# Attention probabilities turned by VectorE in 32x32 squares, with products over 32 keys in eight tiles of TensorE, in a hybrid pooling, convolution and attention block

## The reference

```python
scores = einsum('bnqkgd,bnskd->bnkgqs', qb, kb)   # blocks of 128 queries, 256 keys
in_band = (dist >= 0) & (dist < 128)              # dist = query - key
scores = where(in_band & key_exists, scores - slope * dist, -1e30)
p = softmax(concatenate([scores, sink], -1))[..., :-1]
out = einsum('bnkgqs,bnskd->bnqkgd', p, vb)       # 8 query heads, 2 kv heads of 64
y_attn = out * silu(g_attn)
```

## Time and profile before

| | us |
|---|---|
| median of 3 runs | 1399.54 (1399.27 to 1400.41) |
| profiled execution, its own time | 1400.31 |
| its span | 1398.6 |
| PE busy in the span | 1376.3 (98%) |
| DVE busy | 1189.1 (85%) |
| ACT busy | 553.6 (40%) |
| POOL busy | 389.1 (28%) |

### The profile page before, as it was taken

One profiled execution on the slowest core, in us unless ns is written; L12 is line 12 of the kernel. 1 busy time (PEld: TensorE's weight loads), 2 busy tenths in 40 slices (PEclk: granted clock), 3 DMA queues, 4 the chain that ended last, 5 costly groups with the idle time before them and its releaser, 6 DMA issues.

```text
span 1398.6 us, 21036 instructions
## 1 busy us (share of the span) xinstructions
PE 1376.3 (98%) x7326; PEld 1131.5 (81%) x7326; DVE 1189.1 (85%) x2480; ACT 553.6 (40%) x1435; POOL 389.1 (28%) x592
## 2 busy tenths in 40 slices
PE   6999999999999999999999999999999999999997
PEld 4888888888888888878888888888888888888886
DVE  5887878796978786769899998988999998898886
ACT  5756565655565654512212122111231333333332
POOL 5133324233242423120101101010010455445551
PEclk9999999999999999999999999999999999999999
DMA  9716070616252426363303213032326484555431
GB/s 216 206 45 257 19 273 19 235 75 207 95 199 103 151 106 210 123 118 153 136 16 136 101 66 135 15 135 101 125 113 260 201 264 161 177 180 171 159 108 74
DMA packets 89385, 197.23 MB, mean 141 GB/s; under 512 B 13904, under 2 KB 55248, under 8 KB 81616
## 3 DMA queue, kind: packets, MB, share of 16 engines
q1 hardware_dynamic: 65152, 172.28, 34.9%
q10 hardware_dynamic: 24144, 23.80, 6.5%
HBM read 114.27 MB, written 81.79 MB: 140 GB/s over the span
## 4 chain that ended last, share of the span: by engine, by line
PE 90%; DVE 7%; DMA 1%; ACT 1%; issue 1%; POOL 0%; SPq 0%; POOLq 0%; DVEq 0%; ACTq 0%
PE wide L346 13%; PE wide L347 13%; PE wide L348 13%; PE pair L1186 6%; PE pair L1187 6%; PE pair L1192 6%; PE wide L1186 4%; PE wide L1187 4%; PE wide L1192 4%; DVE m_tail L1967 3%; PE wide L1224 2%; PE pair L1157 2%; PE turn L1144 2%; PE turn L346 2%; PE pair L346 2%; PE pair L348 2%
## 5 line engine op out<-in xcount | busy, mean ns | idle before, releaser
L1967 DVE SCALAR_TENSOR_TENSOR m_tail<-m_tail,m_taps 128x512 f32<-128x512 f32 x480 | 338.4, 750 | 4.6
L108 POOL TENSOR_TENSOR pool_carrier<-pool_carrier 128x1 f32<-128x1 f32 x77 | 29.5, 383 | 692.0 <-DVE m_meanvar L1976 398.4
L1186 PE MATMUL pair<-xT,w_hi 128*128 128x512 f32 x384 | 154.0, 401 | 4.8 <-DVE w_lo L410 4.6
L1187 PE MATMUL pair<-xT,w_lo 128*128 128x512 f32 x384 | 150.6, 392 | 0.0
L1710 POOL TENSOR_TENSOR operand_sums<-m_y 128x512 f32<-128x512 f32 x75 | 102.0, 1360 | 167.8 <-PE wide L348 116.7
L1192 PE MATMUL pair<-xT,w_hi 128*128 128x512 f32 x384 | 147.1, 392 | 0.0
L787 POOL TENSOR_SCALAR a_rows<-a_rows,a_inv 128x128 f32<-128x128 f32 x256 | 111.4, 453 | 75.3 <-DVE a_inv L993 75.3
L346 PE MATMUL wide<-x_first,w_hi 128*128 128x512 f32 x320 | 125.5, 392 | 0.0
L346 PE MATMUL wide<-xT,w_hi 128*128 128x512 f32 x320 | 125.2, 391 | 0.0
L348 PE MATMUL wide<-x_first,w_hi 128*128 128x512 f32 x320 | 124.6, 389 | 0.0
L347 PE MATMUL wide<-x_first,w_lo 128*128 128x512 f32 x320 | 124.6, 389 | 0.0
(11 more groups left out here) (264 smaller groups left out, 3220.0 us busy)
## 6 DMA issues: line engine op xcount, KB each, us to landing
xT_scratch<-xT SPq DMA_DIRECT2D x16, 2048.0 KB, 8.2
x_first<-xT_scratch SPq DMA_DIRECT2D x16, 1024.0 KB, 7.6
xT<-xT_scratch SPq DMA_DIRECT2D x16, 1024.0 KB, 9.0
combo_scratch<-stage SPq DMA_DIRECT2D x28, 512.0 KB, 4.4
m_y<-y_scratch ACTq DMA_DIRECT2D x14, 1024.0 KB, 6.7
xs<-in_x_dram SPq DMA_DIRECT2D x20, 512.0 KB, 8.1
y_scratch<-y_out SPq DMA_DIRECT2D x8, 1024.0 KB, 4.2
y_scratch<-y_out SPq DMA_DIRECT2D x16, 512.0 KB, 2.9
```

The lines of the kernel that those rows point to most:

```text
L1186: nc.tensor.matmul(out, w.hi(c)[:, kk, cols], st.hi[:, kk, :], start=(kk == 0), stop=False)
L1187: nc.tensor.matmul(out, w.lo(c)[:, kk, cols], st.hi[:, kk, :], start=False, stop=False)
L1967: nc.vector.scalar_tensor_tensor(out=conv[:, i, :], in0=h[:, i, j:j + TB], scalar=taps[:, i, j:j + 1], in1=conv[:, i, :], op0=ALU.mult, op ...
```

## The change

The probabilities are no longer transposed by PE. DVE turns them in squares of 32x32 in place of the copies (`turn_probs`, two instructions of 128x512 for a sub-tile, from SBUF to SBUF). Such a turn leaves each block of 32 queries in its own 32 partitions: in partitions 32a to 32a + 31 lie 32 keys, and the columns hold the square of queries. A product can therefore only sum over 32 keys in the partitions of a, where the queries' block is a, so v's rows of the other three blocks of keys must be in those partitions too: SP copies them with 12 DMAs of 64 KB a block (`spread_v`, into `v_spread`). For every 32 queries (`a`, four row tiles, each with its own PSUM bank) and each parity of heads (`odd`, two column tiles), products over 32 keys are made of 32 rows by 64 columns of weights and 64 moving columns. Keys of an earlier 32 come from the own block, keys of a later 32 from the earlier block. On the diagonal square both occur: the product with the earlier block's v is made over the whole square, and the difference of the two v (`step_v`, one POOL operation a block) is multiplied by the square masked to keys not later than the query (`own_diagonal`, four POOL operations a sub-tile, `diag_ready`). That makes 80 products for a sub-tile in place of 16.

The four sums of a sub-tile lie in the two `turn` banks and two of the score banks (`out_banks`), and are copied by four instructions of 128x128 in place of two of 128x256. PE makes the products inside the following gate projection, after its seventh step (`ATTEND_AT = 6`), and the last sub-tile's after q0 of the next block. `scores` of sub-tiles 2 and 3, q0 to q3 and the next products wait for `out_taken`. `o0` to `o3` are no longer uses of the `pair` banks. DVE's output of a sub-tile moves ahead of the second `invert`, and the gate behind it; ACT's tanh moves behind the second exponentials. Masks for the copies are not made any more; one 128x128 mask for the diagonal is.

```diff
+SQ = 32
+ATTEND_AT = 6
+        def spread_v(n):
+            sp.wait_ge(v_ready, n + 1)
+            if n == 0:
+                sp.wait_ge(score_taken, 2)
+            for a in range(SUB):
+                for b in range(SUB):
+                    if a != b:
+                        column, first = (b, 1) if b < a else (b - 1, 0)
+                        sp.dma_start(v_spread[blocks_of_32[a], :, column, :],
+                                     v[blocks_of_32[b], first:first + SUB, :]).then_inc(v_spread_loaded, 16)
...
             store_xT(n, 1)
+            spread_v(n)
...
+        def step_v(n):
+            carrier.pool_wait(pool, v_ready, n + 1)
+            nc.gpsimd.tensor_tensor(v_step, v[:, 1:, :], v[:, 0:SUB, :], ALU.subtract).then_inc(diag_ready, 1)
+
+        def own_diagonal(n, j):
+            pool.wait_ge(pT_done, 2 * (SUB * n + j) + 2)
+            for part in blocks_of_32:
+                mask = not_later[part, part].unsqueeze(1).to_broadcast([SQ, HEADS, SQ])
+                last = nc.gpsimd.tensor_tensor(diagonal[part], squares_of_probs[part, :, part], mask, ALU.mult)
+            last.then_inc(diag_ready, 1)
+            pool.wait_ge(diag_ready, 5 * n + j + 2)
...
             for j in range(SUB):
+                if j:
+                    own_diagonal(n, j - 1)
                 normalise(n, j)
...
-        def pT_copy(m, kv):
-            dve.wait_ge(p_turned, 2 * m + kv + 1)
-            for tile in range(2):
-                last = nc.vector.tensor_tensor(pT[:, tile, kv, :], turn[kv][:], seen[:, tile], ALU.mult)
-            last.then_inc(pT_done, 1)
+        def turn_probs(m, b, kv):
+            dve.wait_ge(probs_ready, 2 * m + kv + 1)
+            need(dve, out_full, m)
+            cols = slice(kv * GROUP * P, (kv + 1) * GROUP * P)
+            nc.vector.transpose(turned_probs[:, cols], rows[:, b, cols]).then_inc(pT_done, 1)
...
+    def out_banks(j):
+        other = [score[:, 2 * t:2 * t + 2].rearrange("p a b -> p (a b)") for t in range(SUB)]
+        return [turn[0][:], turn[1][:]] + (other[0:2] if j < SUB - 1 else other[2:4] if j == SUB - 1 else [proj[0][:], proj[1][:]])
...
+        for kv in range(KV):
+            for column in range(SUB - 1):
+                for a, part in enumerate(blocks_of_32):
+                    keys = blocks_of_32[column if column < a else column + 1]
+                    for odd in range(2):
+                        product(a, kv, odd, v_spread[part, j, column], squares_of_probs[part, heads_of(kv, odd), keys],
+                                kv == 0 and column == 0, False)
+            for a, part in enumerate(blocks_of_32):
+                for odd in range(2):
+                    product(a, kv, odd, v[part, j], squares_of_probs[part, heads_of(kv, odd), part], False, False)
+        pe.wait_ge(diag_ready, 5 * n + j + 2)
+        for kv in range(KV):
+            for a, part in enumerate(blocks_of_32):
+                for odd in range(2):
+                    last = product(a, kv, odd, v_step[part, j], diagonal[part, heads_of(kv, odd)], False, kv == KV - 1)
+        last.then_inc(out_full, 1)
...
             need(pe, score_taken, 2 * (m - 1) + 2)
+            if j > 1:
+                pe.wait_ge(out_taken, m - 1)
...
+        def attending(n, j):
+            def once(kk):
+                if kk == ATTEND_AT:
+                    pe.wait_ge(score_taken, 2 * (SUB * n + j + 1) + 1)
+                    attend(pe, n, j, j)
+            return once
...
                 scores(n, j, turn_v if j == 0 else None)
-                    project(n, f"g{j}", turning(n, j - 1))
-                    attend(pe, m, j - 1, (n, slot(f"o{j - 1}")))
+                project(n, f"g{j}", attending(n, j - 1) if j else None)
```

More of the change, by code:

```diff
@@ L801, in body @@
                 make_seen()
+            else:
+                own_diagonal(n - 1, SUB - 1)
             if not isinstance(n, int) or n < NB - 1:
@@ L860, in body @@
             if not first:
[L861 to L865, removed]
+                act.wait_ge(out_full, SUB * n - 1)
+                for tokens, part in sums_of(SUB - 2):
+                    last = nc.scalar.activation(y[:, :, tokens], part, ACT.Copy)
+                last.then_inc(out_taken, 1)
                 if not final:
@@ L1137, in sums_of @@
-    def sums_of(at):
-        return [bank[:, 0:KV * P] for bank in (pair_bank(at[1]), turn[0])]
-    def turn_probs(pe, m, j, kv):
-        pe.wait_ge(probs_ready, 2 * m + kv + 1)
-        for t in range(GROUP):
-            last = nc.tensor.transpose(turn[kv][:, t * P:(t + 1) * P], probs[:, j % 2, kv * GROUP + t], ident[:])
-        last.then_inc(p_turned, 1)
-    def attend(pe, m, j, at):
-        p = at[1]
-        need(pe, free(p), earlier(*at))
-        pe.wait_ge(pT_done, 2 * m + 2)
-        def product(late, kv, odd, tile, keys, start, stop):
-            queries = halves[late]
-            out = sums_of(at)[late][halves[odd], kv * P:(kv + 1) * P]
-            weights = pT[keys, tile, kv, :].rearrange("p (t o c) -> p t o c", o=2, c=P)[:, :, odd, queries]
-            return nc.tensor.matmul(out, v[keys, j + tile, halves[kv]], weights, start=start, stop=stop)
-        for kv in range(KV):
-            for late in range(2):
+        dve.wait_ge(free(slot("g3")), earlier(NB - 1, slot("g3")) + 1)
@@ new lines, in vector @@
+        dve.wait_ge(out_taken, SUB * NB - 1)
+        nc.vector.tensor_tensor(y[:, :, done], y[:, :, done], gate[:, :, done], ALU.mult).then_inc(constants_made, 1)
+        for kv in range(KV):
+            turn_probs(4 * NB - 1, 1, kv)
+    def gate_last(dve):
+        dve.wait_ge(out_full, SUB * NB)
+        dve.wait_ge(constants_made, 4 + NB)
+        for tokens, part in sums_of(SUB):
+            tokens = slice(tokens.start - P, tokens.stop - P)
+            last = nc.vector.tensor_tensor(y[:, :, tokens], part, gate[:, :, tokens], ALU.mult)
+        last.then_inc(gated, 1)
@@ L1161, in attend @@
                 for odd in range(2):
-                    product(late, kv, odd, late, slice(0, P), kv == 0, False)
+                    product(a, kv, odd, v[part, j], squares_of_probs[part, heads_of(kv, odd), part], False, False)
+        pe.wait_ge(diag_ready, 5 * n + j + 2)
         for kv in range(KV):
-            for late in range(2):
+            for a, part in enumerate(blocks_of_32):
                 for odd in range(2):
-                    last = product(late, kv, odd, 1 - late, halves[late], False, kv == 1)
@@ L1176, in project @@
                 need(pe, score_taken, 2 * SUB * n)
+                if not first_block(n):
+                    pe.wait_ge(out_taken, SUB * n - (1 if name in ("q0", "q1") else 0))
             else:
@@ L1260, in body @@
                 project(n, "k")
-                project(n, "q0", turning(n - 1, 3))
-                attend(pe, 4 * n - 1, 3, (n, slot("o3")))
+                project(n, "q0")
+                attend(pe, n - 1, SUB - 1, SUB - 1)
             final = isinstance(n, int) and n == NB - 1
@@ L2261, in map_u @@
                 last.then_inc(u_mapped, 1)
-        def turn_last(kk):
-            if kk == 2:
-                for kv in range(2):
-                    attention.turn_last(pe, kv)
         def body(m, r):
```

156 lines of the change are left out of this document (71 added, 85 removed).

## The result

The change makes the kernel slower: 1434.66 us (median of four runs, 1434.32 to 1435.1) against 1399.94 (1399.27 to 1400.41) for the kernel before, a ratio of 1.0249 with a 95% interval of 1.0231 to 1.0266. The forecast was 1378. The profiled execution spans 1432.9 us, 34.3 more than the 1398.6 of before.

The account below looks back on a forecast made before the run. PE was taken as the bound: its 10.52 us a block for transposes and products becomes 7.0, 28 us over eight blocks; less waits of 2.5, 2, 0.5, 1.5 and 1.5, plus 1.0, 21 us gained. Forecast 1378 us, range 1364 to 1406.

Parts of the forecast that it names:

- (a): Scores 2 and 3 wait for copies of an earlier attend's output: about 0.15 us, 16 times, 2.5 us (0 to 8).
- (b): The last 32 of an attend's 160 records wait for POOL's masked diagonal: 2 us in all, zero to 29.
- (c): A block's first attend may wait for v's spread by 12 SyncE DMAs: 0.5 us, up to 24.
- (f): In the last block, whatever made POOL late delays the diagonal: 1.5 us, between nothing and 3.
- second rival: New waits, for the diagonal or v's copies, take the gain: 1385 to 1400 us, centre 1393; chance 0.17.
- (d): At a block's start the last x pieces, low parts from DVE, have less time: 1.5 us in all, nothing to 13.5.
- the gain: PE's wait for POOL's probabilities at 599.67 disappears with the transposes: 1.0 us gained.
- first rival: Attend's 160 short records cost too much, losing from 0.014 us each: 1475 us at 0.0275, 1437 at 0.02; chance 0.17.
- Record price: An attend's 160 records take 1.35 us from first to last start, bounds 1.15 and 4.4 us.
- Way in and out: Around its burst of products, each attend pays PE about 0.40 us.
- is not the bound, so nothing is credited: DVE gets some 1 us per sub-tile freer; no gain was counted for it.

Follow-up runs that it names:

- Experiment 1: 64 overwritten products (128 instructions) added ahead of q0 of block 0 in the changed kernel, to move the code borders: 1445.82 us.
- experiment 4: Changed kernel with one product for all four heads of a key-value head (128 columns), half the instructions: 1418.36 us.
- experiment 6: Changed kernel, narrow products, v spread in six transfers, SyncE's queue reordered (spread ahead of store_xT, combinations' stores ahead of y's): 1423.05 us.
- experiment 7: Same six transfers and queue order as experiment 6, but with wide products (all four heads in one): 1396.03 us, ratio 0.9961 to the kernel before.
- experiment 2: Changed kernel with v spread in block 0 alone, later blocks reusing those copies (output not the reference's): 1420.82 us.
- experiment 9: Kernel of experiment 7 with two of the four mask products per attend moved from GpSimd to VectorE: 1400.8 us.
- experiment 11: Kernel of experiment 7 with one of the four mask products per attend moved from GpSimd to VectorE: 1382.04 us, ratio 0.9868 to the kernel before.
- experiment 5: Changed kernel, narrow products, without GpSimd's four mask products per attend (later keys weighted wrongly): 1424.98 us.
- experiment 10: Kernel of experiment 7 with all four mask products per attend on VectorE and none on GpSimd: 1410.06 us.

## Why the prediction was wrong

Forecast and result are 55.4 us apart: 21 us of gain against 34.4 of loss. Of these, 18.2 are stalls for code, which no part of the prediction named, and 12.4 the new waits (a), (b), (c) and (f): 18.9 us where the sum took 6.5. That is the second rival's mechanism at nearly three times what the sum allowed. Another 10.1 are the price of the records with their way in and out, and 14.7 the rest (15.2 measured, where (d) and the gain took 0.5), in the main the half clock. The first rival's 1437 lies near the result by chance: its 0.02 us per record did not come.

*The step that failed* is the sum itself: "28.0 - 2.5 - 2 - 0.5 - 1.5 - 1.5 + 1.0 = 21 us" has no term for bringing PE its instructions. The burst was priced by its records, and 320 instructions were taken to be there when PE wants them. Before, `attend` had 64 instructions, and a projection needs 5.4 us for 48, so a packet of 256 lasts many microseconds and its loading is hidden. Now 256 pass in 1.4 us. Experiment 1 shows that the position of the border decides, experiment 4 that half the instructions have no such stall. The stalls themselves are 18.2 us; experiments 6 and 7 together put the wide products at 27, net of the mask's larger waits. The Trainium skill (Runtime: NRT & Kernel Launch, Instruction fetch mechanics) says that code comes in blocks of 16 KiB by a DMA queue that the sequencer drives itself, and that crossing a border is mostly hidden. The first half agrees with the packets of 16,384 bytes; the second holds for this kernel before, not for a burst like this. The prediction gives no reason for leaving the term out.

*Record price.* "I take 1.35, near the lower end" measured 1.72: 10.7 ns per record, against 8.4. The first rival's border, 0.014 us, was not reached, so this alone left a gain of 17.9 us of the 28. The four starts in 0.02 us of the earlier trace rows were a bad guide to 160 in a row. By the floor of 25 ns of the Trainium skill (TensorE: Matmul & The Clock Gate, Back-to-back issue gap) an `attend` would be 4.0 us: the runs, with 1.72, are against it for matmuls in different tiles. With 128 columns in place of 64 a record costs 14.5 ns, so the columns are not the whole price of the short one: twice the columns, 1.36 times the time.

*Way in and out*: 0.40 taken, 0.35 measured. Right.

*(c) The spread*: "12 DMAs a block at about 0.4 us of issue" is short by a factor of 1.6 to 2.3: 0.65 us each with nothing in the way, 0.9 in the blocks that wait. The row of L189 was for a transfer of another kind; none moved rows inside the on-chip memory. The bound that was named, 24 us, was the better guide; 12.2 came.

*(b) The mask*: half of 1396 ns per product was right to 4% (725 measured), and the waits, 2.6 us where (b) and (f) took 3.5, nearly so, but by luck: they were small because other losses covered them (experiments 2, 4 and 6).

*(a) Scores 2 and 3*: 4.1 us for 2.5. The copies are 0.28 each, as put.

*(d) and the gain*: PEld's waits at a block's start for the low parts are 2.0 us in all (five times), 1.5 put; the 1.0 us at 599.67 is gone. Right.

*Clock.* Nothing in the prediction says that an idle PE also pays afterwards. It costs 16 us here. With the waits for v and the stalls for code out of the way, it went too (experiment 7).

*DVE* "is not the bound, so nothing is credited" was right for this kernel. Once PE's losses were out, VectorE had room for one mask product per `attend` and not for two, which cost it 1.3 us (experiments 9 and 11).

Left open: why the stalls of the 12th `attend` and of the 8th, 16th and 24th with moved code last over 3 us, where others last 1 to 2. In 257.80:263.20 the packet starts at 260.11, 1 us after PE has stopped, and the DMA engines are busy 0.76 of the time; whether that traffic holds the packet was not tried. Open too is what experiment 5 gained beyond its waits.

## What to carry to other kernels

A burst of short matmuls is paid in instructions, not only in columns: count them, and where one packet of code passes in less time than the next takes to come (here 1.4 us against some 3), make each product wider before anything else. Cost a new DMA by a row with the same endpoints and the same company in its queue. And when a loss is taken away, look for the wait that it covered: here the spread covered the mask, and the mask's cure uncovered VectorE.

## What the runs showed of the hardware

- PE resumes 1.3 to 1.7 us after the packet of code that it lacks has landed, and stands still for up to 4.1 us at one border.
- Eight tiles of 32x64: 10.7 ns per record of 64 columns, 14.5 of 128, each with its own weight load.
- A transfer inside the on-chip memory takes 0.65 us of SyncE with an idle queue, and single ones 1.1 to 3.0 us behind stores of 1 and 2 MB.
- A product of two operands in 32x256 takes VectorE 417 ns with no such products on GpSimd (experiment 10, first row), and 649 with two on each engine (experiment 9, the rows after it). GpSimd's own go from 726 to 883 ns. With one on VectorE and three on GpSimd (experiment 11) they are 439 and 803 ns. In time, in experiment 9: VectorE's first starts at 225.80 and takes 0.42 us, GpSimd's first starts at 225.85 and takes 0.96, VectorE's second starts at 226.23 and takes 0.87, so that one that starts while the other engine's runs lasts longer than its usual 0.42 and 0.73:

```profile
L1050 DVE TENSOR_TENSOR a_pT<-a_pT 32x256 f32<-32x256 f32 x128 | 53.3, 417 | 2.4
```

```profile
L823 POOL TENSOR_TENSOR a_pT<-a_pT 32x256 f32<-32x256 f32 x64 | 56.5, 883 | 72.7 <-DVE a_pT L1048 70.8
...
L1055 DVE TENSOR_TENSOR a_pT<-a_pT 32x256 f32<-32x256 f32 x64 | 41.6, 649 | 1.6
```

The Trainium skill (SBUF — State Buffer, Who interferes with whom) says that a VectorE instruction with two inputs there contends with a GpSimd instruction that reads there. The trace agrees, with the times above.
